# Attention with ones columns beside the values, its units and steps in another order, and twelve modulation pieces formed on GpSimd

## The reference, cut to what matters

```python
q = (rms_norm(q_lat, q_norm) @ w_qb).reshape(B, S, H, 64 + 32)   # nope, rope
kv = (rms_norm(kv_lat, kv_norm) @ w_kvb).reshape(B, S, H, 64 + 64)
s = (q_nope . k_nope + q_rope . k_rope) * 96 ** -0.5    # per head, causal, 128 queries a block
p = softmax(s); o = p @ v; y = o @ w_out; x = x + g1 * y
mod = silu(c) @ ada_w[i] + ada_b[i]     # six vectors of 1024: shift, scale, gate, twice
```

## Time and profile before

| | |
|---|---|
| median of three executions | 3023.71 us (3022.76 to 3025.06) |
| the profiled execution, its own time | 3026.73 us |
| its span | 3025.4 us |
| busy in the span | PE 2843.8 us (94%), weight loads 2316.1 (77%), DVE 1716.8 (57%), ACT 1234.9 (41%), POOL 249.5 (8%) |
| mean granted clock of TensorE | 0.979 of 2.4 GHz |

### The profile page before, as it was taken

How to read it: one execution, slowest core, us unless ns; L and a number is a source line. 1 busy time by engine, 2 the same in 40 slices (tenths; PEclk the granted TensorE clock), 3 DMA queues, 4 the chain that set the end, 5 groups by cost and what they waited for, 6 DMA issues and landing times. The chain is left out here.

```text
span 3025.4 us, 36405 instructions
## 1 busy us (share of the span) xinstructions
PE 2843.8 (94%) x14551; PEld 2316.1 (77%) x14551; DVE 1716.8 (57%) x2889; ACT 1234.9 (41%) x2128; POOL 249.5 (8%) x224
## 2 busy tenths in 40 slices
PE   7888999999997989899999998999999998999998
PEld 5766788787886888678877775788788766778886
DVE  6766554445854866543578886533425386654344
ACT  3556322223434344333467775432233345432222
POOL 0000000000003442010000010122100002100000
PEclk8999999999998999899999999999999999999999
DMA  5232344332331111154589994211321214422321
GB/s 227 89 110 88 112 182 154 131 113 89 121 130 39 67 43 43 51 201 143 192 304 366 342 370 165 75 58 48 110 101 46 84 36 132 146 73 86 112 80 67
DMA packets 72098, 387.67 MB, mean 128 GB/s; under 512 B 8235, under 2 KB 9935, under 8 KB 36175
## 3 DMA queue, kind: packets, MB, share of 16 engines
q1 hardware_dynamic: 58512, 349.20, 31.8%
q10 hardware_dynamic: 10382, 26.07, 2.5%
q0 software_dynamic: 3024, 9.98, 0.9%
HBM read 368.43 MB, written 22.03 MB: 129 GB/s over the span
## 5 line engine op out<-in xcount | busy, mean ns | idle before, releaser
L343 DVE TENSOR_TENSOR wlo<-stage,whi 128x1024 fp32r<-128x1024 f32 (+3 forms) x504 | 531.4, 1095 | 352.8 <-ACT whi L355 351.6
L355 ACT ACTIVATE whi<-stage 128x1024 fp32r<-128x1024 f32 (+3 forms) x504 | 440.5, 922 | 222.5 <-PE ps L645 187.1
L645 PE MATMUL ps<-whi,mxhi 128*128 128x512 f32 (+1 forms) x528 | 204.4, 387 | 9.9 <-DVE wlo L343 7.8
L645 PE MATMUL ps<-bxhi,whi 128*128 128x512 f32 x480 | 201.4, 420 | 11.1 <-DVE y0lo L343 4.0
L645 PE MATMUL ps<-whi,mxlo 128*128 128x512 f32 (+1 forms) x528 | 197.8, 375 | 0.0
L645 PE MATMUL ps<-wlo,mxhi 128*128 128x512 f32 (+1 forms) x528 | 197.6, 374 | 0.0
L645 PE MATMUL ps<-bxhi,wlo 128*128 128x512 f32 x480 | 190.9, 398 | 0.0
L645 PE MATMUL ps<-bxlo,whi 128*128 128x512 f32 x480 | 190.1, 396 | 0.0
L343 DVE TENSOR_TENSOR wlo<-more,whi 128x1024 fp32r<-128x1024 f32 (+1 forms) x126 | 142.2, 1170 | 44.4 <-ACT whi L355 43.9
L351 DVE SCALAR_TENSOR_TENSOR part<-stage,small,part 128x256 f32<-128x256 f32 x259 | 151.1, 583 | 9.2
L645 PE MATMUL ps<-gwide 128*128 128x128 f32 x1088 | 135.5, 285 | 14.2 <-POOL gwide L343 11.4
(11 more groups left out here) (597 smaller groups left out, 6308.7 us busy)
## 6 DMA issues: line engine op xcount, KB each, us to landing
stage<-in_gu SPq DMA_DIRECT2D x92, 1024.0 KB, 4.9
stage<-in_ada SPq DMA_DIRECT2D x40, 1024.0 KB, 5.2
more<-in_gu SPq DMA_DIRECT2D x40, 1024.0 KB, 6.9
stage<-in_dn SPq DMA_DIRECT2D x26, 768.0 KB, 4.9
stage<-in_dn SPq DMA_DIRECT2D x19, 1024.0 KB, 6.5
stage<-in_gin SPq DMA_DIRECT2D x16, 1024.0 KB, 4.8
stage<-in_gt SPq DMA_DIRECT2D x16, 1024.0 KB, 4.9
more<-in_dn SPq DMA_DIRECT2D x13, 1024.0 KB
```

What stands on the lines that cost most here:

```text
L343: return e.do.tensor_tensor(out, x, y, op)
L355: return e.do.activation(out, x, f, **kw)
L645: return self.p.do.matmul(out, lhsT, rhs, start=start, stop=stop, skip_group_check=True)
```

## The change

The values are laid out in 192 columns for a pair of heads: 64 of the even head, 64 of ones, 64 of the odd head, so that a block of 128 columns has a head's values and ones. The product of this block (as weights) with the transposed probabilities gives the output already with features in the partitions, and in the other 64 partitions the sums of the probabilities. ACT forms their reciprocal as the exponential of minus the logarithm (`share`), and DVE multiplies (`weigh`), once a head. With that go the sums of the exponentials, the reciprocals, the scaled outputs and the 32 transposes at the end. Scale and sign are put into the maximum instruction, whose result is the exponential's bias. Query blocks go in the order 3, 2, 0, 1; the steps of projection stand in other places, the copy of the transposed probabilities ahead of the exponential, and splits and copies at other steps. Scores and transposes rotate over three banks, two hold the heads' outputs. High and low parts of the output and the first two pieces of `wo` are made among the last units. GpSimd sets the ones and forms the pieces 8 to 19: eight products in place in the staging slot, then sums of 1024, 512 and 256 columns. The waits of SP and PE on these pieces are on GpSimd's semaphore.

```diff
+    def pool_ada(self, i, n):
+
+        g, G = self.g, self.G
+        k, w = self.raw(f"ada{i}", n)
+        r = self.part[n % 2]
+        g.wait_ge(self.load(k)(k), self.A("cond"), self.P(("ada", i, n - 2)))
+        for kk in range(8):
+            ts(g, w[:, kk, :], w[:, kk, :], self.cond[:, kk:kk + 1], None, MUL).then_inc(*G.up())
+        for half in (4, 2, 1):
+            g.wait_ge(G.now())
+            dst, done = (w[:, 0:half, :], ()) if half > 1 else (r, [("raw", k), ("part", i, n)])
+            tt(g, dst if half > 1 else r, w[:, 0:half, :] if half > 1 else w[:, 0, :], w[:, half:2 * half, :] if half > 1 else w[:, 1, :], ADD).then_inc(*G.up(*done))
...
-        p.wait_ge(self.V(("part", i, n)))
+        p.wait_ge(self.G(("part", i, n)) if self.G.has(("part", i, n)) else self.V(("part", i, n)))
...
-        L.V, L.O = self.at("mlav", [P, 4, 1024], 62), self.at("mlao", [P, 4, 1024], 70)
-        L.raw = L.O[:, :, :].rearrange("p a b -> p (a b)").rearrange("p (m n) -> p m n", n=512)
+        L.V = self.at("mlav", [P, 4, 8, 192], 62)
+        ot = self.at("mlao", [P, 4, 512], 74)
+        early = [self.at(n, [P, 2, 512], o) for n, o in (("mlaoa", 52), ("mlaob", 60))]
+        L.OT = [early[i % 2][:, i // 2, :] for i in range(4)] + [ot[:, i, :] for i in range(4)]
+        low = self.at("mlaraw", [P, 4, 512], 84)
+        L.raw = [low[:, i, :] for i in range(4)] + [ot[:, i, :] for i in range(4)]
...
-        return [(h, i) for h in range(16) for i in range(4)]
+        return [(h, i) for h in range(16) for i in (3, 2, 0, 1)]
...
-        yield from self.pe_gemm(("q", g), "wq", [g], L.X, self.normed("nq"), (5, 6))
+        yield from self.pe_gemm(("q", g), "wq", [g], L.X, self.normed("nq"), (5, 6), lead=0 if g else 1)
...
-        self.banks(range(5))
+        self.banks(range(3))
...
-            ps, vacant = self.take(("o", n))
-            p.wait_ge(*vacant, A(free(("t", n))), A(("v", h // 4, 3)))
+            if n % 4 == 0:
+                _, vacant = self.take(("oh", h), at=3 + h % 2)
+                p.wait_ge(*vacant)
+            ps, side = self.bank(("oh", h)), slice(64 * (h % 2), 64 * (h % 2) + 128)
+            p.wait_ge(A(free(("t", n))), A(("v", h // 4, 3)), self.G("ones"))
             for j in range(i + 1):
-                z = self.mm(ps[:, 0:64], L.pt[n % 4][:, j * P:(j + 1) * P], L.V[:, j, h * 64:h * 64 + 64], j == 0, j == i)
+                z = self.mm(ps[:, i * P:(i + 1) * P], L.V[:, j, h // 2, side], L.pt[n % 4][:, j * P:(j + 1) * P], j == 0, j == i)
             z.then_inc(*P_.up(("o", n)))
 
+        def project(count):
+            for _ in range(count):
+                next(more, None)
+
+        places = ((1, 0, 1), (0, 0, 0), (1, 0, 1), (0, 1, 1), (0, 0, 0), (2, 0, 0), (0, 2, 0), (0, 0, 0))
         for n in range(64 + 4):
-            if n % 8 == 0 and n < 56:
-                more = self.mla_project(L, n // 8 + 1)
-            step = more if n % 8 and n < 64 else iter(())
+            if n % 8 == 0:
+                more = self.mla_project(L, n // 8 + 1) if n < 56 else iter(())
             if n < 64:
                 scores(n)
-            next(step, None)
+            project(places[n % 8][0])
             if 3 <= n < 67:
                 turn(n - 3)
-            next(step, None)
+            project(places[n % 8][1])
             if n > 3:
                 values(n - 4)
-            next(step, None)
+            project(places[n % 8][2])
             if n >= 8 and (n - 8) % 4 == 0 and (n - 8) // 4 < 12:
                 self.pe_ada(0, 8 + (n - 8) // 4)
...
-        for m in range(8):
-            ps, vacant = self.take(("ot", m))
-            p.wait_ge(*vacant)
-            for i in range(4):
-                p.wait_ge(A(free(("o", 4 * (2 * m + 1) + i))))
-                z = self.tr(ps[:, i * P:(i + 1) * P], L.O[:, i, m * P:(m + 1) * P])
-            z.then_inc(*P_.up(("ot", m)))
...
-                act(a, L.V[:, t, 256 * n:256 * n + 256], self.bank(use)[:, 0:256], ACT.Copy).then_inc(*A.up(free(use), ("v", n, t)))
+                dst = L.V[:, t, 2 * n:2 * n + 2, :].rearrange("p g (s c) -> p g s c", c=64)[:, :, 0:3:2, :]
+                act(a, dst, self.bank(use)[:, 0:256].rearrange("p (g s c) -> p g s c", g=2, s=2), ACT.Copy).then_inc(*A.up(free(use), ("v", n, t)))
...
+        def share(h):
+            top, low = slice(64 * (h % 2), 64 * (h % 2) + 64), slice(64 - 64 * (h % 2), 128 - 64 * (h % 2))
+            r = L.tmp[2][top, :]
+            a.wait_ge(P_(("o", 4 * h + 3)), *([V(("od", h - 2))] if h > 1 else [V(("nq", "l", 3))]))
+            act(a, r, self.bank(("oh", h))[low, :], ACT.Ln).then_inc(*A.up())
+            a.wait_ge(A.now())
+            act(a, r, r, ACT.Exp, scale=-1.0).then_inc(*A.up(("share", h)))
...
-            if n < 64:
-                w = (units[n][1] + 1) * P
-                c, sl = L.cols[n % 6], L.sl[n % 5]
-                a.wait_ge(V(("nm", n)))
-                act(a, sl[:, 0:w], sl[:, 0:w], ACT.Exp, bias=c[:, 5:6], scale=L.scale, accum_out=c[:, 4:5]).then_inc(*A.up(("e", n)))
-            if n % 8 == 2 and g < 8:
-                self.act_ahead("wq", g, False)
-                self.act_ahead(f"wk{g}", 0, False)
-            if n % 8 == 4 and g < 8:
-                keys(g)
...
                 if u >= 4:
                     a.wait_ge(P_(("o", u - 4)))
                 act(a, L.pt[u % 4][:, 0:w], self.bank(("t", u))[:, 0:w], ACT.Copy).then_inc(*A.up(free(("t", u))))
-            if n % 8 == 3 and g < 8:
-                queries(g)
-            if n > 3:
-                u = n - 4
-                h, i = units[u]
-                a.wait_ge(P_(("o", u)), V(("rl", u)))
-                if u < 4:
-                    a.wait_ge(V(("nk", "l", 1)))
-                act(a, L.O[:, i, h * 64:h * 64 + 64], self.bank(("o", u))[:, 0:64], ACT.Copy, scale=L.cols[u % 6][:, 6:7]).then_inc(*A.up(free(("o", u))))
-            if n % 8 == 7 and g < 7:
+            if n < 64:
+                w = (units[n][1] + 1) * P
+                sl = L.sl[n % 5]
+                a.wait_ge(V(("nm", n)))
+                act(a, sl[:, 0:w], sl[:, 0:w], ACT.Exp, bias=L.cols[n % 6][:, 0:1], scale=-1.0).then_inc(*A.up(("e", n)))
+            if n % 8 == 1 and g < 8:
+                self.act_ahead(f"wk{g}", 0, False)
+            if n % 8 == 2 and g < 8:
+                queries(g, 0)
+            if n % 8 == 4 and g < 8:
+                queries(g, 1)
+            if n % 8 == 6 and g < 8:
+                keys(g, 0)
+                keys(g, 1)
+            if n % 8 == 4 and g < 7:
                 self.act_ahead("wq", g + 1, False)
-        for m in range(8):
-            if m == 0:
-                a.wait_ge(P_(("o", 63)))
-            self.act_high("ot", L.X, m, self.bank(("ot", m))[:, :], P_(("ot", m)))
+            if n > 3 and n % 4 == 3:
+                share((n - 4) // 4)
+            if 56 <= n < 63:
+                self.across_act(L, n - 56)
+            if n in (61, 63):
+                self.act_ahead("wo", 0, n == 63)
+        self.across_act(L, 7)
...
+    def across_act(self, L, m):
+        marks = [self.V(("od", 2 * m)), self.V(("od", 2 * m + 1)), self.P((("k", 7), 0))]
+        if m > 5:
+            marks.append(self.V(("ot", "l", m - 6)))
+        self.act_high("ot", L.X, m, L.OT[m], *marks)
+
+    def mla_pool(self, L):
+        g = self.g
+        g.wait_ge(self.V(("mod", 0, 1)))
+        g.do.memset(L.V[:, :, :, 64:128], 1.0).then_inc(*self.G.up("ones"))
+        for n in range(8, 20):
+            self.pool_ada(0, n)
...
+        def turned(g, part):
+            use, r = (("q", g), 2 * g + 1), L.tmp[part]
+            s = slice(64 * part, 64 * part + 64)
             v.wait_ge(P_(use), V.now())
-            tt(v, r[0:64, :], b[0:64, :], cos[0:64, :], MUL).then_inc(*V.up())
-            tt(v, r2[0:64, :], b[64:128, :], sin[64:128, :], MUL).then_inc(*V.up(free(use)))
-            v.wait_ge(V.now())
-            if g >= 2:
-                v.wait_ge(P_(("s", 8 * (g - 2) + 7)))
-            for h in range(2):
-                s = slice(32 * h, 32 * h + 32)
-                tt(v, L.q[(2 * g + h) % 4][64:96, :], r[s, :], r2[s, :], ADD).then_inc(*V.up(("qe", 2 * g + h)))
+            tt(v, r[0:64, :], self.bank(use)[s, :], (cos, sin)[part][s, :], MUL).then_inc(*V.up(*([free(use)] if part else [])))
+
+        def queries(g, h):
+            v.wait_ge(V.now(), *([P_(("s", 8 * (g - 2) + 7))] if g >= 2 else []))
+            s = slice(32 * h, 32 * h + 32)
+            tt(v, L.q[(2 * g + h) % 4][64:96, :], L.tmp[0][s, :], L.tmp[1][s, :], ADD).then_inc(*V.up(("qe", 2 * g + h)))
...
-        def modulation():
-            for n in range(8, 20):
-                yield from self.dve_ada(0, n)
-                if n % 4 == 0 and n > 8:
-                    self.dve_mod(0, n // 4 - 1)
-
-        more = modulation()
+        def modulation(n):
+            if n in (22, 38):
+                self.dve_mod(0, 2 if n < 32 else 3)
+
+        def weigh(h):
```

(44 more changed lines are left out.)

45 lines of the change are left out of this document (23 added, 22 removed).

## The result

The change makes the kernel a little slower (6.4 us) where a gain of 20.6 us was forecast: a median of 3030.59 us (3026.33 to 3033.67, ten runs) against 3024.14 for the kernel before in the same runs, ratio 1.0016, interval 1.0009 to 1.0024. The forecast was 3003.1 with a range of 2988 to 3018.

A forecast was written before the change was run, and what follows sets the result against it. No engine was full; DVE's late maxima held ACT and PE in the attention rounds. First round -1.0, five rounds -13.5, seventh -3.6 and end -2.5 gave -20.6 us: median 3003.1, range 2988 to 3018.

The forecast's parts named there:

- GpSimd: Step pricing one GpSimd piece: eight products at 0.5 us, sums 4.5 and waits 0.3, together 8.8 us, ends 6.7 and 13.2.
- T: GpSimd's time for one modulation piece in the attention stage, forecast at 8.8 us.
- rival B: GpSimd bounds the rounds: from T = 12.05 two pieces fill one; at 13.2, 26.4 us a round, 3028 in all; chance 0.10.
- the end of the stage: Last units up to the output projection: ACT's work 16.0 plus waits, values and warming, 21.8 us against 24.3, 2.5 gained.
- Stall = T + 4.6 - 12.0: Wait for GpSimd's piece and the load of `wq` before ACT's split: 1.4 us in each of five rounds.
- The passes on the values: Value products on PE with 128 probability columns instead of 64: no gain or cost taken, bounds -0.01 and +0.03 us a pass.
- PE's floor of 19.0 a round: PE's own work in a round of eight attention units, 19.0 us of 24.1; about 1.0 added for semaphore steps.
- DVE at 8.9 a round: DVE's work in an attention round falls from 17.4 to 8.9 us, so its maxima come promptly.
- A: Rival: GpSimd quick enough not to stall, T under 7.4, rounds of 20.0 us, 2996; 2990 at PE's floor; chance 0.22.
- C: Rival: GpSimd blocks DVE's instructions reading two SBUF tiles, +4.0 us a round, 3027 if all on PE's path; chance 0.05.
- D: Rival: waits move but the round stays, the logarithm's wait and three banks delaying the copy; 3015 to 3020; chance 0.11.
- the first paragraph of the prediction: What bounds attention rounds: modulation pieces make DVE's maxima late, delaying ACT and PE; at most 5.1 us a round to gain.

The follow-up runs named there:

- Experiment 4: The changed kernel with DVE's low parts of the output and splits of `wo` one unit later: 3024.17 us, ratio 0.9993 against the kernel before.
- experiment 1: The changed kernel with GpSimd's eight products as one 2048-column instruction, the columns broadcast: 3013.34 us, ratio 0.9964 against the kernel before.
- Experiment 10: The changed kernel with low parts a unit later, GpSimd's products in four of 512 columns, its 1024-column sum in two of 512: 2998.77 us, ratio 0.9909.
- experiment 13: Experiment 10 with more buffers, so that GpSimd's piece n waits for PE's product of n-4, not n-2: 2993.98 us, ratio 0.9893 against the kernel before.
- Experiment 15: The changed kernel with only GpSimd's instructions shortened (four 512-column products, two 512-column sums, then 512 and 256), low parts not moved: 3005.84 us, ratio 0.9935.
- experiment 6: The changed kernel with one wide product, low parts a unit later, and buffers so that piece n waits for PE's product of n-4: 3027.92 us, ratio 1.0000.
- experiment 14: Experiment 13 with longer GpSimd instructions, two products of 1024 columns and one sum of 1024: 3019.06 us, ratio 0.9981 against the kernel before.
- experiment 11: The kernel before, in its old order, with GpSimd forming pieces 8 to 19 by one wide product and three sums: 3025.66 us, ratio 0.9998.
- experiment 12: The kernel before, in its old order, with GpSimd forming pieces 8 to 19 in the short instructions of experiment 10: 3023.22 us, ratio 0.9992.
- experiment 5: The changed kernel with both one wide GpSimd product and DVE's low parts a unit later: 3009.2 us, ratio 0.9934 against the kernel before.
- experiment 7: Experiment 5 with only half the products wide (four of 256 columns, one of 1024): 3014.93 us, ratio 0.9952 against the kernel before.

## Why the prediction was wrong

**The step that failed** is in "GpSimd": "I take 0.5, nearer to the 0.646 row since one input less is read". The product measured 0.92 us by itself and 0.99 on average, at the upper bound of 0.954 and not near 0.5. One input less did not make it cheaper: the sum of two tiles of the same 256 columns took 0.73 by itself. The sums were right (4.5 forecast, 4.45 measured), the waits too. So T was 12.5 on average and not 8.8, and rival B held, with its point put at 12.05: its price at T = 13.2 was 26.4 a round and 3028 us in all, and two pieces of 12.5 make 25 of the 25.6 us that a round took. It had a chance of 0.10. By this step five rounds took 25.6 us in place of 21.4, which is 21 us of the miss of 27.5. The row that was missing is a GpSimd instruction with a column as its operand; the value between the two ends 0.33 and 0.954 was chosen by an argument, not by a row, and the argument pointed to the wrong end. The Trainium skill, "GPSIMD Engine Reference", Performance versus the Vector engine, whose figures had made T near 7 in the prediction, is further off still for the 256 columns in 0.92 to 0.99 us; the wide product (2048 columns in 3.6) lies between its two figures.

**The second step that failed** is the end of the stage: 21.8 us forecast, 32.6 measured, 10.8 us of the miss (the first and the seventh round came out 2.0 and 1.1 us under the forecast, the other way). The prediction added up ACT's work there (16.0) and took ACT for the bound; ACT was busy 21.8, among other things since the logarithms and exponentials of four heads fall within the window (4.9 us) where two (2.6) had been counted. But it is the ring through DVE that sets the time. The prediction had looked at each engine's sum, not at the order in which two engines hand work to and fro. Experiment 4 gets 5.8 us of it back with one unit's delay; its end of 27.0 us is still over the forecast, so the ring is not all of it.

**A step that was right only by luck**: "Stall = T + 4.6 - 12.0". At T = 8.8 it gave rounds of 21.4, and experiment 1 measured 21.2 to 21.5 in four of the five. Experiment 10 takes 19.9 at a T that is 0.9 us longer, where the formula gives 22, so the 12.0 is no property of PE's work. The true chain has 3.8 us from the end of a piece to the split in place of 4.6, and then DVE's low parts and the maximum behind them, which the formula lacked; with long GpSimd instructions the two errors cancelled.

**What was right.** The passes on the values cost nothing more: eight of 128x128 stand at 1.06 us, as forecast:

```profile
178.33 1.06 PE L645 MATMUL ps<-probt,mlav 128*128 128x128 f32 x8
```

PE's floor of 19.0 a round: 18.9 in the free round, 19.2 to 19.7 in experiment 13; the 1.0 us that was added for semaphore steps was not needed. DVE at 8.9 a round (8.0 in the free one), ACT at 12.0 (12.3); ACT's wait before exponentials gone; ACT standing for `wq` in five rounds, though 32.5 us in all. Experiment 15, which mends the failed term alone, lands 2.7 us above the forecast of 3003.1, but by luck: its five rounds are 20.2 us and its seventh 18.9, together 7 us under the forecast, and its end of 32.5 is 10.7 over it.

**Boundaries.** Two of the windows in the earlier trace rows do not begin with the scores that they are named for: those of unit 24 stand at 181.45 us and those of unit 56 at 277.57. The seventh round before was therefore 23.0 us and the end 24.7; their sum, and the forecast, hardly move.

**The rivals.** A (no stall) is what experiment 13 builds: its rounds at the floor, 2994.0, where A said 2990 at PE's floor; its end of the stage is 26.6 us from unit 56, where A took 21.8. B happened. C was small in the change (`wlo` of 512 columns 0.75 us on average from 100 to 300 us, `mlaqh` 0.76, in place of 0.688), where products of 256 columns are short; in experiments 6 and 14 it costs 19 and 25 us, with the lower clock and the waits for loads that come with it. By the Trainium skill, "SBUF — State Buffer", Who interferes with whom, an instruction of DVE with two SBUF inputs that comes second is blocked until GpSimd's has ended; the 2.81 us of `mlaqh` beside a 1024-column sum agree. D (the waits move, the round stays) is refuted: where GpSimd was quick, rounds fell. That the old order was slow because of DVE's pieces, on which the first paragraph of the prediction rests, holds only in part: experiments 11 and 12 take them off DVE, ACT's wait of 53.6 us only falls to 47.4 and 46.4, and they get 0.2 to 1.6 us a round of the 4.7 by which experiment 13's rounds are shorter than the 24.1 before; the rest needs the new order.

**Open** stays why one GpSimd product with a column operand takes nearly as long as a broadcast one of twice its columns, why the remainder of the program after the attention stage is 3.9 us shorter in the profile of experiment 13 than before (2719.3 against 2723.2 us; the other traces lie between 2720.5 and 2724.2), the shares of loads and of the lower clock in experiments 6 and 14, what besides the ring lengthens the end of the stage, and what sets the first round: 19.2 us before and 16.2 in the change, but 19.0 to 21.4 in experiments 1, 5, 10, 13, 14 and 15, and 27.6 and 23.3 in experiments 11 and 12.

## What to carry to other kernels

When work moves to an idle engine, the price of the one instruction form that the trace does not show decides; multiply it by its count before arguing about anything else, price it by the slowest neighbouring row, and check whether two such jobs fill a round. On GpSimd write a row of products with columns as one broadcast two-tensor instruction rather than many with a column operand, but cut it to pieces about as short as DVE's own. In these runs the total time there mattered less than how long one instruction can hold a two-tile instruction of DVE that has a critical one queued behind it. Where two engines hand a tile to and fro in the loop that sets the pace, consume it one step later.

## What the runs showed of the hardware that was not expected

- GpSimd, by itself (medians): 128x256 with a column operand 0.92 us (3.6 ns a column); the same product as a broadcast of two tensors 1.04 us for 512 columns, 1.90 for 1024 and 3.61 for 2048 (experiments 10, 7 and 1), 1.67 ns for each further column. Sums of two full tiles in the change: 0.73, 1.28 and 2.37 us for 256, 512 and 1024 columns, 2.1 to 2.2 ns for each further column.
- The hold goes both ways. Beside a DVE instruction that reads two SBUF tiles GpSimd's own took longer as well: the column product up to 1.75 us, the sum of 256 columns 1.05 (experiments 7 and 10), that of 512 columns 1.60. A mean over both kinds, such as the 0.99, is the price of neither.
- Two DVE low parts of 512 columns, 1.29 us beside the change's 256-column products, took 2.55, 3.33, 4.41 and 5.04 us in the stretches looked at beside GpSimd's instructions of 512, 512, 1024 and 1024 columns (experiments 13, 10, 6, 14). A single one of 0.69 us took up to 4.09, one of 128 columns and 0.29 us up to 3.65 (both in experiment 6).
- Taking a wait away from GpSimd cost 19 us in experiment 6 and gave 4.8, near the noise, in experiment 13: the same edit, with long and with short instructions.
- After a stand of PE of 3.8 to 6.1 us the granted clock was 0.50 to 0.56 for the next 3 us, in all five rounds of the change in which GpSimd sets the pace; where PE's own work then counts, the stand costs more than its length: after the stands of experiment 6 eight value passes took 1.91 us, 1.06 at full clock.
